# Late-awaited stores around the attention, the root taken last in two output stages, and TensorE's feed-forward loop written out

## The reference

```
h  = rms_norm(x, g_pre_mix) * (1 + scale1) + shift1
z  = h @ w_in                                  # 1024 -> 5640 columns
hm = mlstm(z's q,k,v,o,i,f; 4 heads x 128)     # chunked, with states
hd = rms_norm(softmax(q1 k1) v - lam * softmax(q2 k2) v, g_diff)   # 4 heads x 128
merged = sigmoid(gm) * (hm @ w_proj_m) + sigmoid(gd) * (hd @ w_proj_d)
x  = x + gate1 * rms_norm(merged @ w_out, g_post_mix)
h2 = rms_norm(x, g_pre_ffn) * (1 + scale2) + shift2
a, b = split(h2 @ w_up)                        # 2816 each
x  = x + gate2 * rms_norm((gelu(causal_conv3(a)) * b) @ w_down, g_post_ffn)
```

## Time and profile before

| | |
|---|---|
| median of 3 runs | 1828.49 us (1825.04 to 1830.27) |
| profiled execution | 1828.03 us, its span 1826.3 us |
| TensorE matmuls | 1756.1 us busy, 96% of the span, 11470 |
| TensorE weight loads | 1661.9 us, 91% |
| VectorE | 754.7 us, 41% |
| ScalarE | 504.4 us, 28% |
| GpSimd | 149.2 us, 8% |
| granted TensorE clock, mean | 0.99 |
| DMA | 190.4 MB, mean 104 GB/s |

### The profile page before, as it was taken

One profiled execution on the slowest core, in us unless ns is written; L12 is line 12 of the kernel. 1 busy time (PEld: TensorE's weight loads), 2 busy tenths in 40 slices (PEclk: granted clock), 3 DMA queues, 4 the chain that ended last, 5 costly groups with the idle time before them and its releaser, 6 DMA issues. The chain is left out here.

```text
span 1826.3 us, 27364 instructions
## 1 busy us (share of the span) xinstructions
PE 1756.1 (96%) x11470; PEld 1661.9 (91%) x11470; DVE 754.7 (41%) x1011; ACT 504.4 (28%) x813; POOL 149.2 (8%) x231
## 2 busy tenths in 40 slices
PE   6999899999989999999999999999999999999998
PEld 5899878888879889999978899999999999999997
DVE  4522144544431145555544344434434434344345
ACT  4311134434333335341133321211211211211212
POOL 4010000000010014310012210000000000000001
PEclk9999999999989999999999999999999999999999
DMA  9665242332218665433442121111011021011104
GB/s 322 221 199 178 75 165 70 105 110 86 86 47 238 191 189 169 144 82 124 173 155 86 34 93 47 47 47 47 30 64 47 24 70 47 24 58 48 35 34 161
DMA packets 159562, 190.41 MB, mean 104 GB/s; under 512 B 13677, under 2 KB 138109, under 8 KB 159420
## 3 DMA queue, kind: packets, MB, share of 16 engines
q1 hardware_dynamic: 139224, 170.95, 28.9%
q10 hardware_dynamic: 19208, 17.43, 3.0%
q0 software_dynamic: 1008, 0.23, 0.1%
HBM read 146.70 MB, written 41.87 MB: 103 GB/s over the span
## 5 line engine op out<-in xcount | busy, mean ns | idle before, releaser
L158 PE MATMUL ps<-mg_hi,w_hi 128*128 128x352 f32 x1008 | 218.6, 325 | 5.5 <-DVE conv L2724 2.2
L158 PE MATMUL ps<-mg_hi,w_lo 128*128 128x352 f32 x1008 | 217.3, 323 | 0.0
L158 PE MATMUL ps<-mg_lo,w_hi 128*128 128x352 f32 x1008 | 217.0, 323 | 0.0
L158 PEld LDWEIGHTS ps<-mg_hi,w_hi 128*128 128x128 f32 x1008 | 171.4, 189 | 7.2 <-issue 3.8
L158 PEld LDWEIGHTS ps<-mg_hi,w_lo 128*128 128x128 f32 x1008 | 173.1, 188 | 0.0
L158 PEld LDWEIGHTS ps<-mg_lo,w_hi 128*128 128x128 f32 x1008 | 171.2, 188 | 0.0
L2740 DVE TENSOR_TENSOR f_t<-f_t,ps 128x1056 f32<-128x1056 f32 x80 | 100.3, 1254 | 151.2 <-PE ps L158 151.2
L143 DVE TENSOR_TENSOR w_lo<-w_raw,w_hi 128x2048 fp32r<-128x2048 f32 x61 | 141.3, 2316 | 50.5 <-ACT w_hi L139 50.5
L139 ACT ACTIVATE w_hi<-w_raw 128x2048 fp32r<-128x2048 f32 x61 | 116.7, 1913 | 121.0 <-PE ps L158 120.0
L1168 PE MATMUL ps<-acts_hi,w_hi 128*128 128x352 f32 x384 | 133.7, 348 | 9.1 <-PEq L327 4.8
L1284 PE MATMUL ps<-acts_hi,w_hi 128*128 128x352 f32 x384 | 129.4, 337 | 9.2 <-PEq L949 3.9
...
## 6 DMA issues: line engine op xcount, KB each, us to landing
...
```

What stands on the lines that cost most here:

```text
L158: mm = pe.matmul(ps[:, bank + b, 0:TB], w[wi][:, k, j * P:(j + 1) * P], (a_hi, a_lo)[ai][:, k, b * TB:(b + 1) * TB], start=(n == 0), stop= ...
```

## The change

- Input block: the last tile (chunk 5, second half) is computed bank by bank (`last_tile`), DVE evicts each bank into a buffer of its own, `stage_last`, where `w_ada` lay, and SP stores it as the last thing in the block, without waiting for it. The gate row's store and all other waits stand ahead of it. In the attention block SP waits for it at unit 1, and loads head 1 only then; the buffers of head 1 (`z_d1`) are allocated where `stage_last` lies.
- Attention block: ACT squares the last unit ahead of the last z eviction; the last head is normalised in two halves; PE transposes the first half behind the first; DVE evicts one half, ACT the other; SP stores them in two pieces behind all other waits and does not wait for them. SP waits for them in the decode block ahead of the last sequence's value pages, which lie where `cols` lies.
- Mixing output and feed-forward output: `y_gain` multiplies PSUM with the gain ahead of `h_mul` and of the root, and frees the banks; `y_out` multiplies with the root and adds the residual in one operation.
- TensorE's loop over the feed-forward pairs becomes ten pairs in a row. The other engines keep their loops.

```diff
@@ -219,6 +219,8 @@
     z_stored = [[early(f"z_stored{j}{s}") for s in range(2)] for j in range(2)]
+    z_last, z_block = early("z_last_evac"), early("z_last_block")
+    z_late = sem("z_late")
     IN_CHUNKS = 3 * W_MIX // NC_
@@ -240,6 +242,7 @@
         NCOND = DEC_B + 1
+        w_ada_at = nc.sbuf_base
         w_ada = sb("w_ada_chunks", [P, WS, CW])
@@ -252,6 +255,9 @@
+        stage_last = nc.alloc_sbuf_tensor_at("stage_last", [P, T], F32, offset=w_ada_at)
         if_out = at("if_out", 4 * T, [P - TS + H, T])
@@ -442,7 +448,7 @@
-                for c in range(IN_CHUNKS):
+                for c in range(IN_CHUNKS - 1):
                     m = c + 2
@@ -450,11 +456,18 @@
                             gate_store(gate_in(slot))
+                c = IN_CHUNKS - 1
+                load_chunk(sp, c % 2, w_cols(I["w_in"][0], NC_), KT, c + 1)
+                sp.wait_ge(z_evac[0], c + 1)
+                sp.dma_start(ZT[Z_DQ + 2 * c], stage[:, 0, c % 2, :]).then_inc(z_stored[0][c % 2], 16)
+                gate_store(gate_in(2 * c - 1))
                 for j in range(2):
                     for s in range(2):
-                        sp.wait_ge(z_stored[j][s], 16 * IN_CHUNKS // 2)
+                        sp.wait_ge(z_stored[j][s], 16 * (IN_CHUNKS // 2 - j * s))
                 for i in range(4):
                     sp.wait_ge(s_gst[i], 16 * 2)
+                sp.wait_ge(z_last, NTB)
+                sp.dma_start(ZT[Z_DQ + 2 * c + 1], stage_last[:]).then_inc(z_late, 16)
@@ -670,7 +683,14 @@
+                    if c == IN_CHUNKS - 1:
+                        for b in range(NTB):
+                            if b < NTB - 1:
+                                dve.wait_ge(z_block, b + 1)
+                            else:
+                                dve.wait_ge(tile_done, 2 * c + 2)
+                            dve.tensor_copy(stage_last[:, b * TB:(b + 1) * TB], ps[:, 3 + b, 0:TB]).then_inc(z_last, 1)
+                        return
                     dve.wait_ge(tile_done, 2 * c + 2)
@@ -874,13 +894,27 @@
+                def last_tile(c):
...
+                    w = [x[:, c % 2, :].rearrange("p (k n) -> p k n", k=KT) for x in (w_hi, w_lo)]
+                    order = products(KT)
+                    for b in range(NTB):
+                        for n, (k, wi, ai) in enumerate(order):
+                            mm = pe.matmul(ps[:, 3 + b, 0:TB], w[wi][:, k, P:2 * P], (acts_hi, acts_lo)[ai][:, k, b * TB:(b + 1) * TB],
+                                           start=(n == 0), stop=(n == len(order) - 1))
+                        mm.then_inc(z_block if b < NTB - 1 else tile_done, 1)
...
                         pe.wait_ge(z_evac[j], c)
-                        gemm_tile(pe, c % 2, KT, NC_, j, acts_hi, acts_lo, 3 * j)
+                        if (c, j) == (IN_CHUNKS - 1, 1):
+                            last_tile(c)
+                        else:
+                            gemm_tile(pe, c % 2, KT, NC_, j, acts_hi, acts_lo, 3 * j)
                         slot(2 * c - 1 + j)
@@ -907,6 +941,7 @@
     o_cols = sem("o_cols")
+    o_cols_2 = sem("o_cols_act")
     o_stored = sem("o_stored")
@@ -923,8 +958,11 @@
         cur[0] = scope
-        zq, zk, zv = ([sb(f"z_d{x}{i}", [P, SEQ]) for i in range(2)] for x in "qkv")
+        z_d1, z_d0 = ([sb(f"z_d{x}{i}", [P, SEQ]) for x in "qkv"] for i in (1, 0))
+        zq, zk, zv = ([z_d0[n], z_d1[n]] for n in range(3))
         k_tok = sb("k_tok", [P, NCH, P])
...
+        cols = sb("cols", [P, SEQ])
         v_tok = sb("v_tok", [P, NCH, P])
@@ -932,7 +970,6 @@
         sqj = sb("sqj", [P, P], mybir.dt.bfloat16)
-        cols = sb("cols", [P, SEQ])
         row_in = sb("row_in", [H * NCH, 5, P])
@@ -959,12 +996,14 @@
                 load_head(0)
-                load_head(1)
                 sp.dma_start(row_in[:], ROWS.rearrange("q h (c t) -> (h c) q t", c=NCH)).then_inc(n_rows, 16)
...
                     h, i = u // NCH, u % NCH
+                    if u == 1:
+                        sp.wait_ge(z_late, 16)
+                        load_head(1)
                     if i == 1 and 1 <= h < H - 1:
@@ -982,12 +1021,13 @@
                             load_chunk(sp, n % 2, w_cols(I["w_in"][0], col), KT, n - 1)
-                sp.wait_ge(o_cols, 2 * H)
-                sp.dma_start(BRANCH[H - 1], cols[:]).then_inc(o_stored, 16)
                 sp.wait_ge(kv_stored, 32 * H)
-                sp.wait_ge(o_stored, 16 * H)
                 for i in range(2):
                     sp.wait_ge(mz_stored[i], 8 * MZ_TILES)
+                sp.wait_ge(o_cols, 2 * H - 1)
+                sp.dma_start(BRANCH[H - 1, :, 0:512], cols[:, 0:512]).then_inc(o_stored, 16)
+                sp.wait_ge(o_cols_2, 1)
+                sp.dma_start(BRANCH[H - 1, :, 512:SEQ], cols[:, 512:SEQ]).then_inc(o_stored, 16)
@@ -1054,10 +1094,13 @@
                         split_hi(act, n % 2, loads_of(n), TILEM + PER_CHUNK * (u // SPLIT_EVERY))
+                square(UNITS - 1)
                 z_out(MZ_TILES - 1)
-                square(UNITS - 1)
                 act.wait_ge(n_rows_t, 1)
                 act.activation(rows_t[:], ps[:, BZ, 0:5 * H * NCH].rearrange("p (q r) -> p q r", q=5), ACT.Copy).then_inc(n_rows_t, 1)
+                act.wait_ge(o_tr, 2 * H)
+                act.wait_ge(o_stored, 16 * (H - 1))
+                act.activation(cols[:, 512:SEQ], ps[:, BT + 1, :], ACT.Copy, scale=gain_t[:, 2 * H - 1:2 * H]).then_inc(o_cols_2, 1)
@@ -1071,11 +1114,12 @@
                     dve.wait_ge(o_rstd, h + 1)
-                    dve.tensor_tensor(mix[:, h % 2], mix[:, h % 2], q[:, 1, :].unsqueeze(2).broadcast_to((P, NCH, DH)),
-                                      ALU.mult).then_inc(o_norm, 1)
+                    for part in ([slice(0, NCH)] if h < H - 1 else [slice(0, 4), slice(4, NCH)]):
+                        dve.tensor_tensor(mix[:, h % 2, part], mix[:, h % 2, part], q[:, 1, part].unsqueeze(2).broadcast_to(
+                            (P, part.stop - part.start, DH)), ALU.mult).then_inc(o_norm, 1)
...
                 def out_cols(h):
-                    for hf in range(2):
+                    for hf in range(2 if h < H - 1 else 1):
                         dve.wait_ge(o_tr, 2 * h + hf + 1)
@@ -1134,6 +1178,8 @@
                     for hf in range(2):
+                        if h == H - 1:
+                            pe.wait_ge(o_norm, h + hf + 1)
                         for c in range(4):
@@ -1401,6 +1447,7 @@
                         pages(b - 1, v_pg[:, b - 1], I["cache_v"], d_vl)
+                sp.wait_ge(o_stored, 16 * (H + 1))
                 pages(DEC_B - 1, v_pg[:, DEC_B - 1], I["cache_v"], d_vl)
@@ -2336,18 +2383,21 @@
+                def y_gain(t):
+                    r = token_rows(t)
+                    dve.wait_ge(yr_ss, t + 1)
+                    if t >= YS:
+                        dve.wait_ge(yr_stored[t % YS], 16 * (t // YS))
+                        dve.wait_ge(h_s, t - YS + 1)
+                    dve.tensor_tensor(halves(yr[r, t % YS, :]), y_banks(t), halves(gain[r, t // NCH, :]), ALU.mult).then_inc(yr_g, 1)
...
                     dve.wait_ge(yr_rstd, t + 1)
-                    if t >= YS:
-                        dve.wait_ge(yr_stored[t % YS], 16 * (t // YS))
-                        dve.wait_ge(h_s, t - YS + 1)
-                    dve.scalar_tensor_tensor(out=halves(y), in0=y_banks(t), scalar=stat(t, 2), in1=halves(gain[r, t // NCH, :]),
-                                             op0=ALU.mult, op1=ALU.mult).then_inc(yr_g, 1)
                     dve.wait_ge(xr_loaded[t % 2], 16 * (t // 2 + 1))
                     dve.wait_ge(yr_g, t + 1)
-                    dve.tensor_tensor(y, y, xr[r, t % 2, :], ALU.add).then_inc(yr_x, 1)
+                    dve.scalar_tensor_tensor(out=y, in0=y, scalar=stat(t, 2), in1=xr[r, t % 2, :], op0=ALU.mult, op1=ALU.add).then_inc(yr_x, 1)
@@ -2369,6 +2419,7 @@
                     y_stat(t)
+                    y_gain(t)
                     if t:
@@ -2777,23 +2828,27 @@
+                    def y_gain(t):
+                        r = token_rows(t)
+                        dve.wait_ge(fy_ss, t + 1)
+                        if t >= FY:
+                            dve.wait_ge(fy_stored[t % FY], 16 * (t // FY))
+                        dve.tensor_tensor(fy[r, t % FY, :].rearrange("p (b n) -> p b n", b=2), f_banks(t),
+                                          f_gain[r, t // NCH, :].rearrange("p (b n) -> p b n", b=2), ALU.mult).then_inc(fy_g, 1)
...
                         dve.wait_ge(fy_rstd, t + 1)
-                        if t >= FY:
-                            dve.wait_ge(fy_stored[t % FY], 16 * (t // FY))
-                        dve.scalar_tensor_tensor(out=y.rearrange("p (b n) -> p b n", b=2), in0=f_banks(t), scalar=f_stat(t, 2),
-                                                 in1=f_gain[r, t // NCH, :].rearrange("p (b n) -> p b n", b=2),
```

(6 more changed lines are left out.)

## The result

The changed kernel takes 1816.56 us, the median of 4 runs (1816.35 to 1819.97), against 1829.38 us for the kernel before on the same chip (4 runs, 1825.04 to 1831.42). The ratio is 0.9937 with a 95% interval of 0.9915 to 0.9959: faster, by about seven tenths of what was forecast (0.63% beside 0.89%). The profiled execution took 1816.74 us, its span 1815.0; the one of before 1828.03 and 1826.3. The two spans differ by 11.3 us, the forecast's sum was 16.3.

A forecast was written before the change was run, and what follows sets the result against it. TensorE, busy 1756 of the 1826 us span, bounds the kernel, so only its idle or low-clock time can pay. 3.4 - 0.3 + 5.3 + 2.5 + 3.6 + 1.8 = 16.3 us, from 1828.03 to 1811.7; range 1806.5 to 1817.5.

The forecast's parts named there:

- Input block's end: Last tile by banks, store awaited late: next block starts 3.4 us sooner, less 0.3 us at the first scores.
- The change-over: Input block's end: 0.5 us from SyncE's store issue to the next block, so start at 225.65 instead of 229.07.
- Head 0: Attention block's start: head 0's loads, behind the 528 KB store, could come up to 1.3 us late; 0.3 us taken.
- The clock: Attention block's start: idle time ahead of the scores may bring low clock to the first unit; within the 0.3 us.
- rival 1: First attention unit: late head 0 and low clock take about 2 us of the gain; 1813.7 us, chance 0.22.
- Attention block's end: Square first, halves, evictions on two engines, stores awaited later: decode block starts 5.0 to 5.5 us sooner, 5.3 taken.
- rival 4: Decode block's start: low clock goes there too, so better than forecast; 1809 us, chance 0.07.
- Mixing output: Tile 2: gain first, root later saves 1.0 us of TensorE's wait and 1.5 us of half clock; bounds 0 and 3.3.
- the race: Mixing output, tile 2: VectorE's sum starts ahead of GpSimd's h_shift; if GpSimd wins, no 2.5 us, 1814.2, chance 0.12.
- Loop: Feed-forward stage: written out, TensorE's four jumps go, 3.55 us of gaps plus pipeline filling; 3.6 us taken.
- Rival 3: Feed-forward loop: gaps come from the other engines, not the jump, so writing out does nothing; 1815.3 us, chance 0.07.
- rival 5: Feed-forward loop: straight code comes too slowly, some 43 packets each holding TensorE 0.68 us; 1844 us, chance 0.03.

The follow-up runs named there:

- e6: Changed kernel with GpSimd's wait for its own input-block stores moved to SyncE in the attention block; 1818.33 us, ratio 0.9943.
- e8: Changed kernel with GpSimd's wait moved to SyncE and 16 unused products added ahead of the first scores; 1815.25 us, ratio 0.9928.
- e10: e8 with the row, decay and weight loads behind head 0's held until head 0 has landed; 1813.57 us, ratio 0.9925.
- e11: e8 with 19 more unused products around the last eight transposes of the attention block; 1816.68 us, ratio 0.9939.
- e1: Kernel before with only the input block's part of the change; 1829.02 us, ratio 1.0002.
- e2: Kernel before with only the attention block's end changed; 1821.48 us, ratio 0.9965.
- e3: Kernel before with only the gain-first, root-later order in the mixing and feed-forward output; 1825.61 us, ratio 0.9976.
- e4: Kernel before with only TensorE's feed-forward loop written out; 1824.94 us, ratio 0.9982.

## Why the prediction was wrong, and where it was right

**Input block's end, 3.4 - 0.3 us forecast: the step that failed.** Three terms of it.

1. The change-over. I put 0.5 us between SyncE's last issue and the next block, which was true of SyncE and not of the block. I had subtracted SyncE's landing at the attention block's end, got 0.5 us, carried it over, and never listed what the other queues await at the input block's end. GpSimd awaits six stores of its own there and then takes until 225.3; before, SyncE's landing hid it. 2.30 us instead of 3.4. e6 shows it: with that wait gone, 1.43 us behind the last product, the forecast's 1.4, and the same in five more kernels.
2. Head 0. Forecast +0.3 with a bound of 1.3 late; +0.63 in the changed kernel, +1.65 in e6. The small loads behind it take 0.35 us or more of that (e8, e10); the rest isn't settled. The 1.1 us of the first term bought 0.06 in e6, and 0.48 and -0.17 in e8 and e11, which is inside the scatter of single traces.
3. The clock. I wrote that half clock may move to the first unit, gave it part of 0.3 us, and in rival 1 about 2 us, and held against it that "those units are mostly waits". They are not: TensorE is busy for 11.3 of the 13.5 us in the windows above, and the 69 products took 16.25 us in the changed kernel. That is 4.05 us. Rival 1 named the mechanism; its price, for the late head 0 and the clock together, was less than half of the measured 0.63 + 4.05.

From the last input product to the second unit's values the forecast had -3.1 us; it was 27.25 against 24.87, +2.4. That is 5.5 us (1.1, 0.33 and 4.05 by the three terms, so the clock weighs most), more than the whole miss of 5.0; e1 says the same with a ratio of 1.0002.

**Attention block's end, 5.3: right,** 5.47 measured, and e2 alone has the same 4.45 us. The halves, the first transposes under the second half and the eviction on two engines stand in the rows as forecast. No clock gain followed at the decode block (rival 4).

**Mixing output, 1.0 + 1.5: the first right, the second not shown.** The order gives 1.29 us in every kernel that has it (e3: 19.45 against 20.74) and in none without. VectorE won the race: its sum started 0.23 us ahead of h_shift and held it for about 0.9. The Trainium skill (SBUF — State Buffer, section SBUF: two separate sides) has the shared ports as an exclusive lock for the one that starts first. The trace agrees: VectorE's operation keeps its 1.28 us and GpSimd's grows from 1.92 to 2.82, 0.15 us less than if it had done nothing until VectorE's end. The 1.6 us of clock are in the pair of traces, but e2 and e4 have them without the new order, and no trace with the new order lacks them. Whether they are this part's stays open.

**Loop, 3.6: right in kind, 1.0 short.** The gaps between passes held 3.55 us. The unbroken run of 4392 products takes 710.22 us, where I had about 711. I took the idle time of the rows for the price of a jump. It leaves out 0.16 us per jump, because the record of the product ahead reaches that far beyond the time at which the next one is due, and about 0.1 us at the second product, for which I had allowed and then took 0.05 in all: 3.55 + 0.65 + 0.4 = 4.6. Rival 3 falls: e4 changes TensorE's loop alone and keeps the others'. So does rival 5: 4392 straight products have no break. Its 43 instruction packets are what the loop reads over these products; written out, TensorE reads 34. (Its limit of 0.38 us per packet would be 0.30 with the 12.7 us that it uses beside it.) The Trainium skill (Runtime: NRT & Kernel Launch, section Instruction fetch mechanics) says that a taken branch to code outside the two pages at hand has to fetch it before execution goes on, and that kernels therefore prefer written-out code. The traces agree with it: nine packets more and 0.9 to 1.4 us a jump in the loop, neither in the written-out run. That the fetch is what takes the time isn't shown.

**Tail, 1.8: right,** 1.58.

**Not of the change:** -1.41 us ahead of the last input product, where the seventeen traces have 222.85 to 227.01, and +1.99 in the decode stage. They nearly cancel, by chance. I had named the signs of being wrong as a landing at a block end or more half clock; the second came, in the first unit.
